# Three chunks open each later stage, and VectorE turns x's last two groups in whole 32x32 blocks that 16 transfers each carry to their quadrants

## What is computed

```python
x = x + rms_norm(pool_conformer_mixer(rms_norm(x)))   # stage 0
x = x + rms_norm(sq_relu_mlp(rms_norm(x)))            # stage 1: relu(h @ w1)**2 @ w2, d_ff = 8192
x = x + rms_norm(short_conv_mixer(rms_norm(x)))       # stage 2: b * conv3(c * u) @ w_out
x = x + rms_norm(sq_relu_mlp(rms_norm(x)))            # stage 3
# stage 4, from h = rms_norm(x):
q, k, v, z_a, u_b, v_b, z_b, g_a, g_b = split(h @ w_in)
y_a = (attention(rms_norm(q), rms_norm(k), v) * silu(z_a)) @ w_proj_a
y_b = (spatial_gating(gelu(u_b), gelu(v_b)) * silu(z_b)) @ w_proj_b
x = x + (sigmoid(g_a) * y_a + sigmoid(g_b) * y_b) @ w_out
```

## Time and profile before

| | |
|---|---|
| median of three runs | 2673.4 us |
| the profiled execution itself | 2673.97 us |
| its span, first to last instruction | 2672.2 us, granted TensorE clock 1.000 |
| busy: PE, DVE, ACT, POOL | 2665.8, 1960.7, 1289.1, 286.3 us |
| chain of work that ended last | PE 99% |
| instructions of TensorE | 11905 matmuls, 11520 of them of 512 columns |
| weight loads | 1.0 MB each, median 5.0 to 5.3 us from issue to landing |

### The profile page before, as it was taken

One profiled execution on the slowest core, in us unless ns is written; L12 is line 12 of the kernel. 1 busy time (PEld: TensorE's weight loads), 2 busy tenths in 40 slices (PEclk: granted clock), 3 DMA queues, 4 the chain that ended last, 5 costly groups with the idle time before them and its releaser, 6 DMA issues.

```text
span 2672.2 us, 31094 instructions
## 1 busy us (share of the span) xinstructions
PE 2665.8 (100%) x11905; PEld 2207.6 (83%) x11905; DVE 1960.7 (73%) x2706; ACT 1289.1 (48%) x1625; POOL 286.3 (11%) x263
## 2 busy tenths in 40 slices
PE   9999999999999999999999999999999999999999
PEld 7888888888888888888888888888888888888887
DVE  6888867666766787777777676668668869985574
ACT  6875544444444454444544444344455545544452
POOL 4841100000000010000100000000011001000000
PEclk9999999999999999999999999999999999999999
DMA  7555665555655556555556655555555655565554
GB/s 257 189 174 189 209 202 189 189 189 189 205 188 190 199 185 214 190 196 196 190 190 205 204 186 184 198 189 192 190 186 189 208 178 174 175 217 192 189 203 143
DMA packets 268148, 515.57 MB, mean 193 GB/s; under 512 B 8498, under 2 KB 28260, under 8 KB 267492
## 3 DMA queue, kind: packets, MB, share of 16 engines
q1 hardware_dynamic: 267732, 513.34, 57.3%
q10 hardware_dynamic: 272, 0.26, 0.0%
HBM read 511.47 MB, written 2.10 MB: 192 GB/s over the span
## 4 chain that ended last, share of the span: by engine, by line
PE 99%; DVE 0%; DMA 0%; ACT 0%; issue 0%; SPq 0%; DVEq 0%; ACTq 0%
PE bank L839 32%; PE bank L841 32%; PE bank L840 32%; PE bank L890 0%; PE bank L907 0%; PE bank L1062 0%; DMA x_res<-in_x 0%; DMA w_raw<-in_ab_w_in 0%; DVE w_lo L818 0%; PE bank L1076 0%; DVE tap_product L2083 0%; DVE z L2071 0%; PE bank L1048 0%; PE bank L1086 0%; PE bank L1085 0%; PE bank L1027 0%
## 5 line engine op out<-in xcount | busy, mean ns | idle before, releaser
L818 DVE TENSOR_TENSOR w_lo<-w_raw,w_hi 128x1024 fp32r<-128x1024 f32 x950 | 1182.4, 1263 | 439.5 <-ACT w_hi L800 433.0
L800 ACT ACTIVATE w_hi<-w_raw 128x1024 fp32r<-128x1024 f32 x954 | 973.0, 1056 | 615.6 <-PE bank L841 417.9
L839 PE MATMUL bank<-w_hi,A_lo 128*128 128x512 f32 x2432 | 950.6, 391 | 0.9 <-DVE w_lo L808 0.8
L841 PE MATMUL bank<-w_hi,A_hi 128*128 128x512 f32 x2432 | 946.8, 389 | 0.0
L840 PE MATMUL bank<-w_lo,A_hi 128*128 128x512 f32 x2432 | 946.5, 389 | 0.0
L839 PE MATMUL bank<-w_hi,B_lo 128*128 128x512 f32 x1408 | 548.6, 390 | 0.0
L841 PE MATMUL bank<-w_hi,B_hi 128*128 128x512 f32 x1408 | 547.8, 389 | 0.0
L840 PE MATMUL bank<-w_lo,B_hi 128*128 128x512 f32 x1408 | 547.8, 389 | 0.0
L839 PEld LDWEIGHTS bank<-w_hi,A_lo 128*128 128x128 f32 x2432 | 456.6, 188 | 97.7 <-DVE w_lo L808 2.2
L841 PEld LDWEIGHTS bank<-w_hi,A_hi 128*128 128x128 f32 x2432 | 456.5, 188 | 95.2
L840 PEld LDWEIGHTS bank<-w_lo,A_hi 128*128 128x128 f32 x2432 | 456.7, 188 | 93.5
(11 more groups left out here) (176 smaller groups left out, 991.6 us busy)
## 6 DMA issues: line engine op xcount, KB each, us to landing
w_raw<-in_ffn_w SPq DMA_DIRECT2D x256, 1024.0 KB, 5.3
w_raw<-in_w_in SPq DMA_DIRECT2D x88, 1024.0 KB, 5.0
w_raw<-in_sc_w_in SPq DMA_DIRECT2D x48, 1024.0 KB, 5.1
w_raw<-in_ab_w_out SPq DMA_DIRECT2D x16, 1024.0 KB, 5.0
w_raw<-in_sc_w_out SPq DMA_DIRECT2D x16, 1024.0 KB, 5.0
w_raw<-in_w_out SPq DMA_DIRECT2D x16, 1024.0 KB, 5.0
w_raw<-in_ab_w_in SPq DMA_DIRECT2D x26, 512.0 KB, 4.9
w_raw<-in_ab_w_in SPq DMA_DIRECT2D x8, 1024.0 KB, 5.1
```

The source lines that it names most:

```text
L800: e.activation(w_hi[:, s % SPLIT_SLOTS, :], raw_step(s), ACT.Copy).then_inc(hi_made, 1)
L818: e.tensor_tensor(w_lo[:, slot, :], raw_step(s), w_hi[:, slot, :].bitcast(F32), ALU.subtract).then_inc(lo_made, 1)
L839: e.matmul(ps, lo[:, kt, tok], wh, start=first, stop=False)
L841: ins = e.matmul(ps, hi[:, kt, tok], wh, start=False, stop=last)
```

## The change

In each of the stages 1 to 4 three chunks open the stage instead of two: steps 0 to 11 are their first halves (x groups 0 and 1), 12 to 15 group 2 and 16 to 19 group 3 of the first two chunks, and 20 to 23 the third chunk's second half. So the first chunk ends with step 17 (before: 11), the second with step 19 (before: 15), the third with step 23 (as before). The third chunk uses banks 4 and 5.

TensorE no longer transposes x's group 2. DVE transposes groups 2 and 3, each with two instructions on all 128 partitions (`turn_quads`), which turn every 32x32 block in its own quadrant of partitions; 16 transfers for each group (`move_x`), issued by SP between its weight loads, carry the blocks to the quadrants where they belong. ACT and DVE cast group 2 at step 10 and group 3 at step 14.

What depends on a chunk's end moves. The MLP's hidden transposes of block 0 take 7 steps instead of 8, and stand at steps 19 to 25 with the cast at 26, and 27 to 33 with the cast at 34 (before: 13 to 20 with the cast at 21, and 22 to 29 with the cast at 30). In stage 2 the turn of the first c x u goes from steps 16 to 23 to steps 20 to 27, and that of the first b from 24 to 31 to 28 to 35. In stage 4 the turns of q and k go from steps 15, 21, 27 and 35 on to 21, 26, 31 and 36 on, each over 5 steps (before: 6, 6, 5, 5).

```diff
+BY_VECTOR = (2, 3)
+Q = 32
+X_HALVES = {2: 10, 3: 14}
...
-QK_TURNS = [(3, 6), (5, 6), (3, 5), (3, 5)]
+QK_TURNS = [(3, 5), (6, 5), (7, 5), (4, 5)]
...
-                for half in range(2):
-                    SEQ += [(c, 4 * half + i) for c in (first, first + 1) for i in range(4)]
-                rest = first + 2
+                SEQ += [(first + n, i) for n in range(3) for i in range(4)]
+                for half in range(2, 4):
+                    SEQ += [(c, 2 * half + i) for c in (first, first + 1) for i in range(2)]
+                SEQ += [(first + 2, i) for i in range(4, 8)]
+                rest = first + 3
             while rest < end:
...
+        def hidden_steps(b):
+            return 7 if b == 0 else TURN_STEPS
+
         TURN_AT = {}
         for layer in range(2):
             free = 0
             for b in range(NB):
                 for j in range(2):
                     TURN_AT[layer, b, j] = max(free, S_END[up_chunk(layer, b, j)] + 1)
-                    free = TURN_AT[layer, b, j] + TURN_STEPS + 1
+                    free = TURN_AT[layer, b, j] + hidden_steps(b) + 1
...
-        x_T = conv_out_flat[:, GK * TOK:2 * GK * TOK].rearrange("p (k t) -> p k t", k=GK)
+        by_block = {2: conv_out_flat[:, 0:GK * TOK], 3: z_flat[0]}
+        by_feature = {2: conv_out_flat[:, GK * TOK:2 * GK * TOK], 3: conv_out_flat[:, 0:GK * TOK]}
...
+        THIRD = [STAGE[p] + 2 for p in range(1, 5)]
+
         def main_bank(c, tt):
-            return bank[2 * (c % 2) + tt]
+            return bank[4 + tt if c in THIRD else 2 * (c % 2) + tt]
...
+            def move_x(p, g, q):
+
+                if q == 0:
+                    e.wait_ge(x_turned.sem, x_turned.of(p, g))
+                    if g == 3:
+                        e.wait_ge(x_moved[2], 256 * p)
+                n = GK * TOK // 4
+                for f in range(4):
+                    e.dma_start(by_feature[g][f * Q:(f + 1) * Q, q * n:(q + 1) * n],
+                                by_block[g][q * Q:(q + 1) * Q, f * n:(f + 1) * n]).then_inc(x_moved[g], 16)
...
+            moves = [(S0[STAGE[p]] + split, p, g, q) for p in range(1, 5)
+                     for g, splits in ((2, (4, 4, 6, 6)), (3, (8, 8, 10, 10))) for q, split in enumerate(splits)]
             for n in range(RAW_SLOTS, LOADS):
+                while moves and moves[0][0] < STEPS_PER_LOAD * (n - RAW_SLOTS + 1):
+                    move_x(*moves.pop(0)[1:])
                 load_weights(n)
...
+            if i == 0 and c in THIRD:
+                e.wait_ge(lo_cast.sem, lo_cast.of("pre", THIRD.index(c) + 1, 1, 1, 1))
+            elif i == 0 and c >= 2:
+                for before in (c - 4, c - 2) if c - 2 in THIRD else (c - 2,):
+                    for tt in which:
+                        sem, value = taken(before, tt)
+                        e.wait_ge(sem, value)
...
-            pe_mlp(e, turn_x, 0)
+            for c, i in matmul_steps(e, 1):
+                pass
...
-                if (c, i) == (C_L1 + 1, 0):
-                    turn_x(2, 2)
...
-                e.wait_ge(x_turned.sem, x_turned.of(p))
+            def hi_moved(p, g):
+
+                e.wait_ge(x_moved[g], 256 * p)
                 for h in two:
                     for k in (2 * h, 2 * h + 1):
-                        kt = GK * (NG - 1) + k
-                        ins = e.activation(halves["A"][0][:, kt, :], x_T[:, k, :], ACT.Copy, scale=par_col(PRE_COL[p], kt))
-                    ins.then_inc(hi_cast("pre", p, NG - 1, h), 1)
+                        for tt in tiles:
+                            ins = e.activation(half_kt(halves["A"][0], g, k, tt), moved_x(g, k, tt), ACT.Copy,
+                                               scale=par_col(PRE_COL[p], GK * g + k))
+                    ins.then_inc(hi_cast("pre", p, g, h), 1)
...
-                if (c, i) == (STAGE[p] + 1, 0):
-                    hi_x(p, 2)
-                if (c, i) == (STAGE[p] + 1, 1):
+                n = POS[c, i] - S0[STAGE[p]]
+                if n == 5:
                     statistics(p)
-                if (c, i) == (STAGE[p], 4):
-                    hi_turned(p)
+                for g in BY_VECTOR:
+                    if n == X_HALVES[g]:
+                        hi_moved(p, g)
...
-                        if POS[c, i] == TURN_AT[layer, b, j] + TURN_STEPS:
+                        if POS[c, i] == TURN_AT[layer, b, j] + hidden_steps(b):
...
-            def turn_last(p, n):
-
-                if n == 0:
-                    e.wait_ge(x_made.sem, x_made.of(p - 1, NG - 1, 1))
-                tok = slice(32 * n, 32 * n + 32)
-                for q in range(4):
-                    feat = slice(32 * q, 32 * q + 32)
-                    ins = e.transpose(x_T[feat, :, :].rearrange("p k (t c) -> p t k c", t=NT)[:, :, :, tok],
-                                      x[tok, :, D - CH:].rearrange("p t (k c) -> p t k c", k=GK)[:, :, :, feat])
-                if n == 3:
-                    ins.then_inc(x_turned(p), 1)
-
-            def lo_turned(p):
+            def turn_quads(p, g):
+
+                for tt in tiles:
+                    e.wait_ge(x_made.sem, x_made.of(p - 1, g, tt))
+                    out = by_block[g].rearrange("p (f t k c) -> p t k f c", f=4, k=GK, t=NT)[:, tt, :, :, :]
+                    ins = e.transpose(out, x[:, tt, g * CH:(g + 1) * CH].rearrange("p (k f c) -> p k f c", f=4, k=GK))
+                ins.then_inc(x_turned(p, g), 1)
...
                 lo_tile(p, 1, 1)
+                turn_quads(p, 2)
                 split_to(e, split_lo, at, f + 4)
                 for tt in tiles:
                     update(p - 1, 3, tt)
                 split_to(e, split_lo, at, f + 5)
...
-                if (c, i) == (STAGE[p] + 1, 0):
-                    lo_x(p, 2)
-                n = POS[c, i] - S0[STAGE[p]] - 3
-                if 0 <= n < 4:
-                    turn_last(p, n)
-                if (c, i) == (STAGE[p] + 1, 3):
-                    lo_turned(p)
+                n = POS[c, i] - S0[STAGE[p]]
+                if n == 3:
+                    turn_quads(p, 3)
+                for g in BY_VECTOR:
+                    if n == X_HALVES[g]:
+                        lo_moved(p, g)
...
-                if part == 2 and j < NG:
-                    if i == 0:
-                        e.wait_ge(dve_took.sem, dve_took.of(c - 1, 1))
-                        if j > 0:
-                            e.wait_ge(short_made.sem, short_made.of(j - 1, SHORT_K - 1, GK - 1))
-                    ins = turn_blocks(e, z[:, z_slot("c", j), :, :], short_in[:, :, SPAD:], i)
...
+                for j in range(NG):
+                    made = C_L1 + 3 * j + 1
+                    n = POS[c, i] - S_END[made]
+                    if 0 <= n < TURN_STEPS:
...
+                        ins = turn_blocks(e, z[:, z_slot("c", j), :, :], short_in[:, :, SPAD:], n)
+                        if n == TURN_STEPS - 1:
+                            ins.then_inc(c_turned(j), 1)
                 for k in range(NG):
-                    n = POS[c, i] - S0[C_L1 + 3 * k + 3] - (1 if k == NG - 1 else 0)
+                    n = POS[c, i] - S0[C_L1 + 3 * k + 3] - (4 if k == 0 else 1 if k == NG - 1 else 0)
...
+            ins = turn_blocks(e, z[:, z_slot("h", layer, b, j), :, :], h_T, n, hidden_steps(b))
+            if n == hidden_steps(b) - 1:
```

More of the change, by code:

```diff
@@ L241, in small_banks @@
     for key in turn_order():
-        if key[0] == "pre" and key[1] > 0 and key[2] == NG - 1:
+        if key[0] == "pre" and key[1] > 0 and key[2] in BY_VECTOR:
             continue
@@ L472, in build @@
                                    ([(g, tt) for tt in tiles for g in gs] if 0 in gs else [(g, tt) for g in gs for tt in tiles])])
-        x_turned = signal("x_turned", [(p,) for p in range(1, 5)])
+        x_turned = signal("x_turned", [(p, g) for p in range(1, 5) for g in BY_VECTOR])
+        x_moved = {g: semaphore(f"x_moved{g}") for g in BY_VECTOR}
         tap_done = signal("tap_done", DVE_TAPS)
@@ L818, in split_lo, with moved_x, half_kt @@
             e.tensor_tensor(w_lo[:, slot, :], raw_step(s), w_hi[:, slot, :].bitcast(F32), ALU.subtract).then_inc(lo_made, 1)
+        def moved_x(g, k, tt):
+            return by_feature[g].rearrange("p (q t k c) -> p t k q c", t=NT, k=GK, c=Q)[:, tt, k, :, :]
+        def half_kt(v, g, k, tt):
+            return v[:, GK * g + k, tt * P:(tt + 1) * P].rearrange("p (q c) -> p q c", c=Q)
         def step_matmuls(e, c, i, which, done, between=None):
@@ L859, in wait_step @@
             e.wait_ge(lo_cast.sem, max(lo_cast.of(*halves_key(c, i, tt)) for tt in which))
-            if i == 0 and c >= 2:
-                for tt in which:
-                    sem, value = taken(c - 2, tt)
-                    e.wait_ge(sem, value)
+            if i == 0 and c in THIRD:
[5 more added lines that the diff above has]
+                        e.wait_ge(sem, value)
         def matmul_steps(e, stage):
@@ L1006, in pe_program @@
```

(23 more changed lines are left out.)

21 lines of the change are left out of this document (5 added, 16 removed).

## The result

The changed kernel takes 2696.5 us (median of five, 2695.7 to 2701.0) against 2673.6 before (2673.1 to 2674.3): a ratio of 1.0091, 95% interval 1.0079 to 1.0102. The forecast was 2682.4 with a range to 2690: the sign was right, the time lies outside the range, and the loss is 22.9 us where 9.0 were forecast.

The account below looks back on a forecast made before the run. TensorE was taken to bound the kernel, never standing still behind the start. The terms -3.7 + 0.6 + 8.1 + 0.3 + 3.7 = +9.0 us gave 2682.4 us (+0.34%), with a range of 2678 to 2690.

Parts of the forecast that it names:

- The turns taken from TensorE (-3.7): Stage openings: four turns of x's group 2 leave TensorE, 0.93 us each, saving 3.7 us.
- the transposes (+0.6): Stage openings: VectorE's 128-partition transposes, 0.7 us each, make step 4's weight half slightly late; 0.6 us over four stages.
- The transfers (0): SP's 32 small transfers a stage, 0.42 us each to issue, cost nothing, with about 3 us of cover.
- The bound of 1 us: Transfers: if an issue cost 1 us, each lot takes 8 us and the four stages lose about 40.
- The following through: Stage 1's opening: transfer lots and weight loads traced in time until TensorE wants group 3's halves at step 14.
- The MLP's tile (0,1) (+8.1): Stages 1 and 3: the cast comes behind step 35's split, so TensorE waits 4.0 to 4.1 us at step 34; 8.1 us.
- rival 3: TensorE's clock falls behind each 4 us standstill, at least 2.7 us more each, 2687.8 up to 2693; chance 10%.
- Stage 2 (+0.3): Four pairs of b's pieces between steps 32 and 35 fill VectorE and make step 39's split late by 0.3 us.
- stage 4 (+3.7): VectorE's turns of q and k fall behind from step 29 to step 39, making TensorE 3.7 us late.
- Stage 2's bound of 1 us: The lateness at step 39 in stage 2 was put at 1 us at most.
- rival 4: Transposes or transfers are dear: quadrants in turn give 44 us, 2726; issues of 1 us some 40, 2722; chance 8%.

Follow-up runs that it names:

- a2: The changed kernel with 4 transfers a group in place of 16, so stale values in x's groups 2 and 3; 2688.1 us.
- b2: Changed kernel with gain row behind transfers, hidden tiles in 6 steps, q/k turns spread, group 3's casts and stage 2's first b turn two steps sooner; 2670.2 us.
- a1: The changed kernel with the gain row's load in stages 1 and 3 issued some 20 steps later, behind all transfers of x; 2690.8 us.
- c1: The changed kernel with group 3's casts two steps sooner in ScalarE's and VectorE's order, step 12 instead of 14; 2692.6 us.
- a4: The changed kernel with stage 4's turns of q and k spread over steps 21 to 51 instead of 21 to 40; 2694.9 us.

## Why the prediction was wrong, step by step

**The turns taken from TensorE (-3.7) and the transposes (+0.6): right.** Openings without other trouble are 0.8 to 1.0 us shorter (stages 2 and 4; a2 and b2 in all four), for 0.78 forecast: of the 0.15 us lost in each by the sum, little came. A transpose on 128 partitions takes 0.69 us for 0.7.

**The transfers (0): wrong, and the step that failed.** It cost 13.5 us, 4.8 of them by the clock behind the waits. Three links of it:
- The price. "A small one took SP 0.42 us to issue" was one row. In lots the median is 0.59, and one begins 0.63 behind another. "SP is not full" turned on that number: at 0.42 a lot and a load fill 3.8 of 5.44 us, at 0.63 they fill 5.6. The bound of 1 us was there, the 40 us of it too, but nothing between: a queue costs nothing up to the point where it is full, and then all at once, and that point, some 0.6 us, was the number to look for.
- The following through. It had the second lot end at 265.9 (269.4), group 2 landed by 271 (273.99), and group 3's first lot with the next load behind it issued by 274.6 (279.6), with 3 us of cover. All of the 5 us lost on the way are SyncE's own time: 3.5 us by the end of the second lot, and 2.0 for the third lot and the load behind it (5.6 us instead of 3.6); the landing itself took half a us less than forecast (4.6 us behind the second lot, for 5.1), since the gain row's delay was in the sum. That delay is the other condition, seen rightly and then covered by too low a price: a1 took only the gain row away, a2 only the issue time, and one was enough, or nearly.
- What is queued behind. I followed the load to TensorE (step 14, 1.4 us late) but not to ScalarE's order, where group 3's casts stand behind the next load's halves. That gave the larger wait, 2.8 us, and c1, where it is 0.3 us or nothing, shows that it was their place.

**The MLP's tile (0,1) (+8.1): the mechanism and its size right (8.2 of wait), its price too low.** What follows a wait is part of its price: 3.9 us of clock and restart for both. That was rival 3, at 10%, in kind; its size, at least 2.7 us a wait, was too high for step 34, where 1.9 came. I had given it little because "no row shows a pause of 4 us", which is a reason not to know, not a reason against. The Trainium skill, page "TensorE: Matmul & The Clock Gate", section "The HAM clock gate (the "warmup" mystery)", has the clock go down when TensorE has idled. By that rule the traces agree: it fell at 24 of 26 waits of 2.05 us or more.

**Stage 2 (+0.3) is 0.81, stage 4 (+3.7) is 4.07: right in mechanism, a little low.** a4 and b2 took each away by moving the pieces named. Stage 2's bound of 1 us held. TensorE waits there once, at step 39; its whole list from 990 to 1300 us is

```profile
PE bank L872 <- DVE w_lo L845: 0.5, 1, 0.5
```

(0.5 us are listed, and by the starts the matmuls come 0.8 later). From the split of step 35 to that of step 39 VectorE takes 4.2 us more than before, where the sum had 3.9, and the split of step 35 itself comes 0.2 later against TensorE.

**The rivals were treated as if only one could come.** What came is the forecast with rival 3 at every wait of over 2 us and a smaller form of rival 4 in two openings. 9.0 + 13.5 + 3.9 + 0.6 is the 27.0 of the ledger. The range was put together from one rival at a time and ended at 2690.

## What to carry to other kernels

Before a queue is called "not full", find the price per issue at which it fills, and take that price from issues that stand back to back; if it lies inside the bounds, it is a case with a chance of its own. Follow what comes late through the order of each engine that it passes, since the largest wait may be for something that merely stands behind it. And where TensorE has never paused, price a pause with the clock behind it: at the 24 waits here, of 2.05 to 6.4 us, the lower clock cost another 1.4 to 3.1 us (an estimate, half of the time at 1.2 GHz that lies behind the wait). The better remedy is to let no such pause happen, which here took five small edits of the order.
